# Recurrent pairs of a hybrid encoder: packing first, score products and masks by direction on two banks, the group norm's chain and the next score product begun sooner

## The reference, cut to what matters

```python
def rwkv7_mixer(h, w_in, mu, w0, w2, a0, a2, k_k, k_a, r_k, gn_w, gn_b, w_out):
    ...
    def step(S, inp):
        r_t, w_t, k_t, v_t, a_t, b_t = inp
        sa = jnp.einsum('dbhij,dbhj->dbhi', S, a_t)
        S = S * w_t[..., None, :] + sa[..., None] * b_t[..., None, :] + v_t[..., None] * k_t[..., None, :]
        return S, jnp.einsum('dbhij,dbhj->dbhi', S, r_t)
    ...
    _, ys = lax.scan(step, S0, xs)
    y = jnp.transpose(ys[:, 0] + jnp.flip(ys[:, 1], axis=0), (1, 0, 2, 3))
    mean = jnp.mean(y, axis=-1, keepdims=True)
    var = jnp.mean(jnp.square(y - mean), axis=-1, keepdims=True)
    y = ((y - mean) * lax.rsqrt(var + GN_EPS)).reshape(B, L, E) * gn_w + gn_b
    ...
    y = y + (bonus[..., None] * v.reshape(B, L, H, N)).reshape(B, L, E)
    return (y.astype(h.dtype) * jax.nn.silu(g)) @ w_out
```

## Time and profile before

| | us |
|---|---|
| median of 3 runs | 4234.78 (4233.78 to 4238.66) |
| the profiled execution | 4246.76, of which the span 4245.0 |
| PE busy | 3499.3 (82% of the span) |
| DVE busy | 2101.5 (50%) |
| ACT busy | 1136.3 (27%) |
| granted PE clock over the span | 0.895 |

### The profile page before, as it was taken

One profiled execution on the slowest core, in us unless ns is written; L12 is line 12 of the kernel. 1 busy time (PEld: TensorE's weight loads), 2 busy tenths in 40 slices (PEclk: granted clock), 3 DMA queues, 4 the chain that ended last, 5 costly groups with the idle time before them and its releaser, 6 DMA issues. The chain is left out here.

```text
span 4245.0 us, 96984 instructions
## 1 busy us (share of the span) xinstructions
PE 3499.3 (82%) x41452; PEld 2472.3 (58%) x41452; DVE 2101.5 (50%) x4017; ACT 1136.3 (27%) x2764; POOL 0.2 (0%) x4
## 2 busy tenths in 40 slices
PE   4978888889888859899979797387788888888977
PEld 2556766676676526666655454144466666766664
DVE  3253454354444235767761599613545544454432
ACT  2132333333233113333320200101233333333320
POOL 0000000000000000000000000000000000000000
PEclk7989998888898979999989898698899989989988
DMA  3111111110110211111102111020000000000002
GB/s 141 55 62 41 54 45 34 48 63 27 38 62 32 88 69 32 38 30 45 30 20 80 51 45 45 8 92 30 27 18 8 18 17 13 13 13 18 16 24 93
DMA packets 65781, 178.67 MB, mean 42 GB/s; under 512 B 9104, under 2 KB 22544, under 8 KB 65424
## 3 DMA queue, kind: packets, MB, share of 16 engines
q1 hardware_dynamic: 53472, 144.02, 10.2%
q10 hardware_dynamic: 11952, 29.04, 1.9%
HBM read 157.30 MB, written 15.73 MB: 41 GB/s over the span
## 5 line engine op out<-in xcount | busy, mean ns | idle before, releaser
L1624 DVE SCALAR_TENSOR_TENSOR RBF<-bank,ID 128x256 bf16<-128x256 f32 x480 | 194.0, 423 | 402.7 <-PE bank L610 396.4
L949 PE MATMUL bank<-BY,W 128*128 128x384 f32 x1024 | 340.4, 496 | 48.0 <-DVEq L1697 35.3
L808 PE MATMUL bank<-BH,W 128*128 128x384 f32 x1024 | 341.6, 489 | 6.9 <-ACT HZ L1210 6.6
L949 PEld LDWEIGHTS bank<-BY,W 128*128 128x128 f32 x1024 | 198.7, 195 | 188.4 <-DVEq L1697 35.9
L1031 PE MATMUL bank<-BH,W 128*128 128x384 f32 x768 | 261.4, 505 | 38.2 <-DMA W<-in_cf_w_in 22.9
L949 PE MATMUL bank<-BX,W 128*128 128x384 f32 x640 | 219.1, 500 | 66.4 <-DVE BX L1936 66.1
L808 PEld LDWEIGHTS bank<-BH,W 128*128 128x128 f32 x1024 | 191.3, 191 | 136.3 <-issue 15.5
L1671 DVE SCALAR_TENSOR_TENSOR CACC<-CU,CV,CACC 128x512 f32<-128x512 f32 x480 | 254.7, 611 | 0.0
L1031 PEld LDWEIGHTS bank<-BH,W 128*128 128x128 f32 x768 | 151.2, 198 | 148.3 <-issue 29.8
L771 PE MATMUL bank<-BD,W 128*128 128x384 f32 x512 | 228.5, 575 | 0.0
L730 PE MATMUL bank<-BH,W 128*128 128x384 f32 x512 | 213.0, 546 | 8.9 <-DVE BH L1936 8.9
(11 more groups left out here) (264 smaller groups left out, 6476.1 us busy)
## 6 DMA issues: line engine op xcount, KB each, us to landing
W<-in_mod_w SPq DMA_DIRECT2D x96, 512.0 KB, 3.6
W<-in_rw_w_in SPq DMA_DIRECT2D x68, 512.0 KB, 3.7
W<-in_hy_w_in SPq DMA_DIRECT2D x32, 512.0 KB, 7.0
x_scratch<-BX ACTq DMA_DIRECT2D x32, 384.0 KB, 3.4
W<-in_cf_w_in SPq DMA_DIRECT2D x24, 512.0 KB, 3.4
SQ<-x_scratch ACTq DMA_DIRECT2D x24, 384.0 KB, 4.2
W<-in_rw_w_out SPq DMA_DIRECT2D x16, 512.0 KB, 3.7
W<-in_hy_w_out SPq DMA_DIRECT2D x8, 512.0 KB, 3.5
```

What stands on the lines that cost most here:

```text
L808: mm = pe.matmul(pj(h), W[:, s, k, :], BH[:, k, tok(h)], start=(k == 0), stop=(k == KT - 1))
L949: mm = pe.matmul(pj(h), lhs(k), rhs(k, h), start=(k == 0), stop=(k == nk - 1))
L1624: v.scalar_tensor_tensor(RBF[:, d, :, :], xout(d), -1.0, bc(ID2[:, 1 if r < NBF else 0, :], GC), ALU.mult, ALU.add).then_inc(ir_ready, 1)
```

## The change

It rewrites the two lists, and splits the steps `L` and `ab` by direction.

- In a group `packA` comes before `u4`, `rate1` and `y3` instead of behind them; the eighths of the value projection stand earlier; `V` (transposes of the values) stands between `x4` and `u4`.
- `ab` writes direction 0 to SC[1] and direction 1 to SC[0], and signals after each. `L` becomes an early step behind `ab`: for each direction DVE masks 256 columns and makes L1B, then LNB for both directions, so that ACT no longer copies LNB. LN in fp32 is written in `packR`, behind rk's signal.
- Between pairs `mean` moves ahead of `r4`, the square (`msq`) ahead of `r5`, `var` ahead of `r6`; `ab` and `L` of the next pair's first group stand ahead of `r7`, and `varb` and `norm` behind it. The three last instructions of the norm are a step of their own (`gated`).

```diff
-GROUP_ORDER = ("v0", "L", "rhs0", "z1", "sa0", "packR", "v1", "x0", "p0", "modA", "KS", "u0", "rhs1", "y0", "v2", "mask0", "x1", "sa1", "mask1",
...
-               "decay2", "v5", "u3", "rhs3", "y2", "decay3", "exp", "v6", "x4", "sa3", "rate0", "v7", "u4", "modS", "p3", "rate1", "y3", "V", "packA",
-               "modR", "ab")
+GROUP_ORDER = ("rhs0", "z1", "v0", "sa0", "packR", "x0", "v1", "p0", "modA", "KS", "u0", "v2", "rhs1", "y0", "mask0", "x1", "v3", "sa1", "mask1",
...
+               "v7", "p2", "decay2", "u3", "rhs3", "y2", "decay3", "exp", "x4", "V", "sa3", "rate0", "packA", "u4", "modS", "p3", "rate1", "y3",
+               "modR", "ab", "L")
...
-              "y3", "ks", "r4", "r5", "ksb", "r6", "r7", "mean", "rate0", "rate1", "var", "varb", "packA", "norm", "ab")
+              "y3", "ks", "mean", "r4", "ksb", "msq", "r5", "rate0", "packA", "var", "rate1", "r6", "ab", "L", "spread", "r7", "varb", "norm", "gated")
...
+                if q:
+                    pe.wait_ge(s_read, q * 3)
                 pe.wait_ge(ab_ready, q + 1)
                 for d in range(2):
                     for c in range(GC):
                         for rows in H2:
-                            mm = pe.matmul(SC[1][rows, (d * GC + c) * CH:(d * GC + c + 1) * CH], AR[rows, p, d, c, 0, :], BK[rows, d, c, 0, :],
+                            mm = pe.matmul(SC[1 - d][rows, c * CH:(c + 1) * CH], AR[rows, p, d, c, 0, :], BK[rows, d, c, 0, :],
                                            start=True, stop=True)
-                mm.then_inc(abm_full, 1)
+                    mm.then_inc(abm_full, 1)
...
-            if step == "L":
-                act.wait_ge(ln_ready, q + 1)
-                act.copy(LNB[:, :, :, :], LN[:, :, :, :]).then_inc(lb_ready, 1)
...
                 v.tensor_tensor(BK[:, :, :, 1, :], ch4(KD), ch4(EX[:, 1, :, :]), ALU.mult).then_inc(rk_ready, 1)
+                m4 = lambda ap: ap.rearrange("p d c t -> p (d c) t")
+                v.tensor_tensor(m4(LN[:, :, :, :]), m4(DN), bc(ID2[:, 0, :], 2 * GC), ALU.add).then_inc(ln_ready, 1)
             if step == "L":
 
-                v.wait_ge(abm_full, q + 1)
-                ab = SC[1][:, :].rearrange("p (d c t) -> p d c t", d=2, c=GC)
-                eye, m4 = bc(ID2[:, 0, :], 2 * GC), lambda ap: ap.rearrange("p d c t -> p (d c) t")
-                C.link(v.tensor_tensor(DN, ab, bc(MAB[:, :, :], GC, 2), ALU.mult))
-                v.tensor_tensor(m4(LN[:, :, :, :]), m4(DN), eye, ALU.add).then_inc(ln_ready, 1)
-                v.scalar_tensor_tensor(m4(L1B[:, :, :, :]), m4(DN), -1.0, eye, ALU.mult, ALU.add).then_inc(l_ready, 1)
+                eye = bc(ID2[:, 0, :], GC)
+                for d in range(2):
+                    v.wait_ge(abm_full, q * 2 + d + 1)
+                    C.link(v.tensor_tensor(DN[:, d, :, :], SC[1 - d][:, 0:GT].rearrange("p (c t) -> p c t", c=GC), bc(MAB[:, d, :], GC), ALU.mult))
+                    v.scalar_tensor_tensor(L1B[:, d, :, :], DN[:, d, :, :], -1.0, eye, ALU.mult, ALU.add).then_inc(l_ready, 1)
+                for d in range(2):
+                    v.tensor_tensor(LNB[:, d, :, :], DN[:, d, :, :], eye, ALU.add).then_inc(lb_ready, 1)
```

More of the change, by code:

```diff
@@ L106, in __exit__ @@
         c.n = 0
-PER = {"act": {"gate": 0}, "dve": {"mod": 0, "gates": 0, "gate": 0, "pair": 73, "hy": 188, "cf": 64, "out": 0}}
+PER = {"act": {"gate": 0}, "dve": {"mod": 0, "gates": 0, "gate": 0, "pair": 76, "hy": 188, "cf": 64, "out": 0}}
 def trunk_program(nc, a, out, layers=(0, 1, 2, 3)):
@@ L576, in pe_group @@
             if step == "z1":
[L578 removed]
                 for d in range(2):
+                    pe.wait_ge(l_ready, q * 2 + d + 1)
                     for c in range(GC):
@@ L599, in pe_group @@
                     if r == 0:
-                        pe.wait_ge(lb_ready, q + 1)
+                        pe.wait_ge(lb_ready, q * 2 + d + 1)
+                    if r == NBF:
+                        pe.wait_ge(ln_ready, q + 1)
                     if r < NBF:
@@ L757, in pe_between @@
                 elif not ahead:
-                    if step not in ("q", "norm"):
+                    if step not in ("q", "msq", "spread", "norm", "gated"):
                         pe_chunk(pe, J, NSG - 1, step)
@@ L1168, in act_between @@
                     act.copy(TT[:, 1, :].rearrange("p (x e) -> p x e", e=HEAD), RT[:, 0, :].unsqueeze(2).to_broadcast([P, 12, HEAD])).then_inc(ks_b, 1)
-                elif step == "mean":
+                elif step == "msq":
                     act.wait_ge(yc_ready, J + 1)
-                    act.activation(TT[:, 1, :], YA[:, :], ACT.Square).then_inc(ysq_ready, 1)
+                    act.activation(TT[:, 0, :], YA[:, :], ACT.Square).then_inc(ysq_ready, 1)
                 elif step == "var":
@@ L1174, in act_between @@
                     act.activation(RT[:, 1, :], SQB[:, 0:12], ACT.Sqrt, scale=1.0 / HEAD, bias=EPSV[:, 1:2]).then_inc(var_rt, 1)
-                elif step == "varb":
+                elif step == "spread":
                     act.wait_ge(var_rc, J + 1)
                     act.copy(TT[:, 1, :].rearrange("p (x e) -> p x e", e=HEAD), RT[:, 1, :].unsqueeze(2).to_broadcast([P, 12, HEAD])).then_inc(var_b, 1)
-                elif step not in ("q", "bonus", "norm"):
+                elif step not in ("q", "bonus", "mean", "varb", "norm", "gated"):
                     act_chunk(act, J, NSG - 1, step)
@@ L1492, in dve_between @@
                     v.sem_inc(norm_read, 1)
+                elif step == "gated":
                     C.link(v.tensor_scalar(YA[:, :], YA[:, :], VG[:, 0:1], VG[:, 1:2], ALU.mult, ALU.add))
@@ L1593, in dve_group @@
                 v.wait_ge(bt_full, q * 2 + 2)
+                rate = C.n
                 C.mark(v.scalar_tensor_tensor(AR[:, p, :, :, 0, :], ch4(blocks(KK, s)), -1.0, ch4(EX[:, 2, :, :]), ALU.mult, ALU.mult))
+                C.wait(rate)
                 v.tensor_tensor(BK[:, :, :, 0, :], ch4(AA), ch4(EX[:, 1, :, :]), ALU.mult).then_inc(ab_ready, 1)
```

6 lines of the change are left out of this document (3 added, 3 removed).

## The result

The changed kernel takes 4175.97 us (median of 4 runs, 4169.22 to 4183.89), the kernel before 4234.28 beside it: a ratio of 0.9861, with a 95% interval from 0.9842 to 0.9880. The interval lies clear of 1, so the change is faster, by 1.4%, and the time is inside the forecast's range; but the gain is 58 us where 127 were forecast. Between the two profiled executions it is 71.4 us of span, because the profiled execution of the kernel before was 12 us above its median; these 71.4 are what the traces can account for.

The account below looks back on a forecast made before the run. PE's queue sets the pace, with time lost to idling and its lower clock. Tails 119 + 11 - 6 (handovers) + 3 (first pairs) = 127 us from 4246.8 gives 4120, 12 less for the median: 4108 us, range 4070 to 4190.

Parts of the forecast that it names:

- The tail, up to `v1`: End of a pair: eighths cover the norm's chain at full clock; PE idles only 0.8 us, at `v0` for the norm.
- The tail, `packR`: End of a pair: `KS` waits for `packR`, which stands behind the gate on DVE; PE idles 1.2 us.
- the tails' 119: 14 ends of pairs, each 8.5 us shorter, 119 us in all; bounds for a tail 9.3 and 5.
- A layer 3 pair: Sign in the profile: a layer 3 pair should take about 127 us instead of 136.4.
- Group 0 into group 1: Handover: sooner `packA` and earlier value eighths cancel, so `KS` starts about when it did: 0, between -1 and +1.5 us.
- Group 1 into group 2: Handover: `packA` starts when `y3` ends, `ab` 1.5 us sooner, `KS` 1.4 us sooner; 8 × 1.4 = 11 us gained.
- In layer 0 the two handovers together: `ab` still waits for `modR` and comes 1 to 2 us later; cost 0.8 us a pair, 6 us in all.
- `L` by direction and LNB on DVE: 1.15 us more DVE work in each of 48 groups, 55 us, costed at nothing beyond the waits already counted.
- nothing waits for ACT there: ACT loses a copy per group that it had idled for; no wait for ACT was expected there.
- The lower clock stays: Rival: waits at `v0` and `KS` hold PE at 1.2 GHz as far as `u0`; 71 us gained, 4164; chance 0.15.
- Added DVE work on the path: Rival: DVE's added work counts in every group, taking 55 of the 127 us; 72 us gained, 4163; chance 0.11.
- Slower: Rival: at 32 inner handovers `L` costs 3.95 us each; with lower clock on top 4289 us; chance 0.06.

Follow-up runs that it names:

- run 1: Changed kernel with VectorE's (DVE's) pair loop written out seven times instead of a loop with a jump: 4104.37 us, ratio 0.9689.
- Run 8: Changed kernel with group 0's value eighths and `V` back at their old places: 4046.34 us with DVE's loop written out, 4101.18 us with the loop.
- Run 6: Changed kernel, DVE's loop written out, with `L` on one bank and LNB copied by ACT as before the change: 4177.73 us, ratio 0.9863.
- runs 1 and 2: run 1, and the changed kernel with its loop kept, moved by memsets put ahead of everything else: 60 give 4121.49 us, 128 give 4172.64 us.

## Why the prediction was half right

*The tail, up to `v1`: right.* The norm's chain is covered by the eighths (the mean moved up by four of them and a spread, not by two as the part on the change says), the lower clock is gone from it, and the wait for the norm is 0.90 us for a forecast of 0.8.

*The tail, `packR`: the step that failed.* "`KS` needs `packR`, which stands behind the gate: DVE took ... 1.63 from L1600 to the end of L1602" joins two distances that were each read inside one iteration, with nothing between them, although the loop's jump lies there. In 12 of the 14 tails 3.2 us of fetching lie there. Even the usual price of the jump was left out, though the prediction's own figures have it: from the gate's end at 3322.43 to `L` at 3323.05 are 0.62 us. Moved by 60, with 0.68 at this place, `KS` waits 1.70 us instead of the 1.2 forecast. Against run 1 a looped tail of layer 3 loses 4.40 - 1.13 = 3.27 us of waiting, 3.68 - 1.96 = 1.72 on `KS` at the lower clock and 0.2 on `u0`, 5.2 in all. Where the jump has only its usual price (moved by 60) the 14 tails give 438.3 - 313.8 = 124.5 us, and written out a tail takes 21.84 us where the prediction's layout ends after 21.8; the tails' 119 was the right size for a kernel without that wait. The whole time then falls by 4236.1 - 4121.5 = 114.6 us by the medians (130.8 between the profiled executions), and by 131.7 written out, for the 127 of the sum. A layer 3 pair, 126.3 to 127.0 us written out, takes the 127 that were forecast. What was missing was not in the list of added operations but in their number: I costed what 16 more instructions take, and not where the loop's body ends up.

A rule spoke of this, and I hadn't weighed it. The page "Runtime: NRT & Kernel Launch" of the Trainium skill, section "Instruction fetch mechanics", says that the instruction memory of most engines holds two pages of 256 instructions, fills sequentially, and that a taken branch to a target outside this window has to wait for a fetch. The runs agree that the place decides (4121.49 us moved by 60, 4172.64 moved by 128). They differ in the size of a page, with packets of 8 KB that come 126 to 133 instructions apart, and they add the price, 3.1 to 5.8 us a jump.

*Group 0 into group 1: a sum of two large terms taken for nothing.* The prediction had `packA` sooner and the earlier eighths, by which `rate0` begins 2.6 us later, cancel, "0, between -1 and +1.5 us"; `V`'s new place isn't in it. Their sum was in that range (27.46 against 26.7 us in layer 3 and about 31.3 against 30.0 in layer 0, both written out), but on its bad side; with the loop, behind a tail that ends at the lower clock, it is up to 28.5 in layer 3 and 32.4 in layer 0, 1.4 us a handover more than before on average. Run 8 takes it apart: the eighths and `V` at their new places cost 3.3 us in layer 3 up to `KS`, and 1.3 more in `KS` itself, which runs at the lower clock; the rest of the change at this place gives 2.5. The cost of 16 such handovers, 21.8 us, is the second part of the shortfall; 11.7 us that came from the stretch behind the last `KS` of a pair, not forecast, pay half of it back. In layer 0 these stretches vary between 51 and 59 us from pair to pair in both kernels, so I don't name a cause for them.

*Group 1 into group 2: the first link right, the size wrong.* Layer 3 gives 2.7 us instead of 11. At the pair of the earlier trace rows `ab` starts 1.65 us behind `y3` instead of 2.92, close to the 1.5 us forecast, but `KS` only 0.85 us sooner, for 1.4; the recurrence between them runs nearer the lower clock (0.47 us for four matmuls that took 0.30), and so does the `KS` of group 1, which the row counts (26.9 us in layer 3 for 24.0). In layer 0 the two handovers together cost 4.0 us for a forecast of 6, 11.5 lost at the first and 7.5 won at the second. That the row's 10.2 comes near 11 is chance.

*`L` by direction and LNB on DVE: costed at nothing, and not shown by itself.* The work was over-sized: DVE's busy time rose by 35.9 us, not 55. Run 6 takes it away, but gives ACT its copy again, so the 73 us there belong to both. That "nothing waits for ACT there" was wrong. In the kernel before `rhs0` waited for ACT's queue at every handover from group 0 to group 1:

```profile
PE bank L662 <- ACTq L1133: 26.6, 16, 1.7
```

In the changed kernel this wait is gone, and `z1`'s wait for L1B stands in its place (1.31 us in the first rows of run 8, which are run 1's). `KS` starts 5.5 us behind the start of `ab` before and 5.7 in those rows, so the wait that went gave nothing there.

*The rivals.* "The lower clock stays" gave 71 us, the gain of the profiled runs, but by luck, through a mechanism that runs 1 and 2 refute: with waits of 0.90 and 1.13 or 1.70 us in the tail, `KS` takes 1.96 and 1.97 us, the full clock, as soon as the fetch is gone. "Added DVE work on the path" gave 72, and runs 1 and 2, which keep all that work, gain 132 and 115. "Slower" needed 4 us a handover; the 32 handovers cost 0.4 each on average (21.8 - 10.2 = 11.6 us). None had the jump in it.

## What to carry to other kernels

When an edit adds instructions to a loop that stays a loop, count the body on each engine and look at the instruction queues' packets in the profile: a jump that was free can begin to fetch, and a jump that lies on the critical path pays for it every time. An idle stretch with the releaser "issue" at a loop's end, in all iterations but the last, is the mark; moving the loop by some instructions at an idle place tells in one run. Writing it out tells less by itself, since it also takes out the instructions that handle registers. And when two effects of a change cancel in an estimate, undo one of them: the 58 us of run 8 had been hidden in a zero.

## What the runs showed of the hardware that I had not expected

- DVE's jump back costs several sizes here: 0.22 us between gate and copy with no jump, 0.7 with a jump that fetches nothing, 3.2 to 3.4 where one packet starts in the gap; in the kernel before, moved by 36, 3.1 to 3.3 us in layer 3, with one packet, and 5.3 to 5.8 in layer 0, with two.
- Memsets ahead of everything else change the time by +50 us (36 of them, kernel before) and by -54 us (60, changed kernel); 128 change it by 3 us, within the spread of the runs.
- Written out, the kernel before has layer 3 tails that are mostly 3 us shorter, of which only 0.5 us is the wait at `z1`; the rest is matmuls that ran at 1.2 GHz and run at 2.4 now (`v1` 2.53 us, then 1.56).
